# Spreading the four input deviations: one float32 matmul, or two of a rounded part and a rest

## The reference

```python
def rmsnorm(x, w):
    xf = x.astype(jnp.float32)
    y = xf * lax.rsqrt(jnp.mean(xf * xf, axis=-1, keepdims=True) + EPS)
    return (y * w.astype(jnp.float32)).astype(x.dtype)

def trunk(x, p):
    for layer in range(DEPTH):
        i = layer // 2
        h = rmsnorm(x, p['norm_w'][layer, 0])
        ...
        x = x + rmsnorm(m, p['norm_w'][layer, 1])
        h = rmsnorm(x, p['norm_w'][layer, 2])
        f = conv_ffn(h, p['ffn_w_in'][layer], p['ffn_conv_w'][layer], p['ffn_conv_b'][layer], p['ffn_w_out'][layer])
        x = x + rmsnorm(f, p['norm_w'][layer, 3])
    return x
```

## Time and profile before

| what | value |
|---|---|
| median of 3 runs | 1378.53 us (1378.49 to 1379.01) |
| the profiled execution | 1378.49 us |
| its span in the trace | 1376.7 us |
| PE busy | 1354.2 us, 98% of the span |
| DVE busy | 821.7 us, 60% |
| ACT busy | 641.7 us, 47% |
| POOL busy | 635.7 us, 46% |
| spread matmuls (L455) | 8 records, 592 ns each in the median |

### The profile page before, as it was taken

The page is one execution under the profiler, slowest core; times in us unless marked ns, Lnnn a source line. Parts: engine busy times, 40 slices in busy tenths (PEclk is TensorE's granted clock), DMA queues, the critical chain, the costliest instruction groups (busy, mean ns, idle before and its releaser), DMA issues.

```text
span 1376.7 us, 16583 instructions
## 1 busy us (share of the span) xinstructions
PE 1354.2 (98%) x6642; PEld 1122.5 (82%) x6642; DVE 821.7 (60%) x977; ACT 641.7 (47%) x1017; POOL 635.7 (46%) x304
## 2 busy tenths in 40 slices
PE   7999999999999999999999999999999999999997
PEld 6878767878898888888889877897898888888886
DVE  5657696760078998885001654477279998883003
ACT  6553885553345454444223475553545444443221
POOL 2344693226514554445454253563525544445550
PEclk9999999999999999999999999999999999999998
DMA  6332101123313332332333323211322333332321
GB/s 210 94 94 78 37 1 39 31 89 96 92 56 118 103 92 92 100 96 85 100 98 94 101 62 93 92 32 46 121 79 92 99 100 92 94 99 86 98 84 62
DMA packets 36765, 117.89 MB, mean 86 GB/s; under 512 B 3856, under 2 KB 8336, under 8 KB 36688
## 3 DMA queue, kind: packets, MB, share of 16 engines
q1 hardware_dynamic: 35744, 114.38, 26.8%
q10 hardware_dynamic: 944, 2.45, 0.6%
HBM read 114.58 MB, written 2.10 MB: 85 GB/s over the span
## 4 chain that ended last, share of the span: by engine, by line
PE 90%; DVE 4%; ACT 3%; POOL 2%; issue 0%; DMA 0%; DVEq 0%; ACTq 0%
PE bank L327 27%; PE bank L329 26%; PE bank L328 26%; PE bank L1350 1%; PE bank L1353 1%; PE bank L1174 1%; PE bank L1881 1%; PE bank L1378 1%; PE bank L1899 1%; POOL ebuf L1010 1%; ACT ebuf L1098 1%; DVE xres L583 1%; POOL ebuf L1006 1%; PE bank L1600 0%; PE bank L418 0%; DVE xw_lo L602 0%
## 5 line engine op out<-in xcount | busy, mean ns | idle before, releaser
L310 POOL TENSOR_TENSOR wlo<-raw,whi 128x1024 fp32r<-128x1024 f32 (+2 forms) x215 | 525.3, 2457 | 660.9 <-ACT whi L304 660.6
L327 PE MATMUL bank<-xw_hi,whi 128*128 128x512 f32 (+1 forms) x1344 | 510.4, 380 | 9.9 <-DVE xw_lo L602 8.2
L329 PE MATMUL bank<-xw_hi,wlo 128*128 128x512 f32 (+1 forms) x1344 | 500.3, 372 | 0.0
L328 PE MATMUL bank<-xw_lo,whi 128*128 128x512 f32 (+1 forms) x1344 | 500.0, 372 | 0.0
L304 ACT ACTIVATE whi<-raw 128x1024 fp32r<-128x1024 f32 (+2 forms) x217 | 221.1, 1024 | 208.7 <-DMA raw<-in_fout 113.6
L327 PEld LDWEIGHTS bank<-xw_hi,whi 128*128 128x128 f32 x1344 | 254.2, 189 | 60.0 <-issue 14.0
L328 PEld LDWEIGHTS bank<-xw_lo,whi 128*128 128x128 f32 x1344 | 254.1, 189 | 47.4 <-issue 3.5
L329 PEld LDWEIGHTS bank<-xw_hi,wlo 128*128 128x128 f32 x1344 | 253.9, 189 | 45.5
L555 DVE RECIPROCAL small<-small 128x2 f32<-128x2 f32 (+1 forms) x12 | 2.0, 169 | 328.1 <-ACT small L487 318.2
L660 DVE SCALAR_TENSOR_TENSOR cbuf<-ubuf,par,cbuf 128x510 f32<-128x510 f32 x100 | 170.8, 1708 | 3.5
L656 DVE SCALAR_TENSOR_TENSOR cbuf<-ubuf,par,cbuf 128x510 f32<-128x510 f32 x100 | 156.7, 1567 | 0.9 <-ACT cbuf L690 0.6
(11 more groups left out here) (251 smaller groups left out, 1432.8 us busy)
## 6 DMA issues: line engine op xcount, KB each, us to landing
raw<-in_fin SPq DMA_DIRECT2D x88, 512.0 KB, 3.6
raw<-in_fout SPq DMA_DIRECT2D x32, 448.0 KB, 3.3
raw<-in_gin SPq DMA_DIRECT2D x25, 512.0 KB, 3.6
raw<-in_hin SPq DMA_DIRECT2D x24, 512.0 KB, 3.6
raw<-in_hout SPq DMA_DIRECT2D x16, 512.0 KB, 3.6
raw<-in_fout SPq DMA_DIRECT2D x16, 512.0 KB, 3.5
raw<-in_gout SPq DMA_DIRECT2D x8, 512.0 KB, 3.7
xres<-in_x SPq DMA_DIRECT2D x8, 256.0 KB, 6.3
```

Of the source, the lines that this page charges most:

```text
L310: engine.tensor_tensor(wlo[s][:, 0:n], raw[s][:, 0:n], whi[s][:, 0:n].bitcast(F32), ALU.subtract).then_inc(w_lo, 1)
L327: first = nc.tensor.matmul(out_ap, wh, ah, start=start, stop=False)
L328: nc.tensor.matmul(out_ap, wh, al, start=False, stop=False)
L329: return first, nc.tensor.matmul(out_ap, wl, ah, start=False, stop=stop)
```

## The change

The four reciprocals are split as the weights are: DVE rounds them to float32r (`parts_r[:, 0:4]`), subtracts that from the reciprocals (`parts_r[:, 4:8]`), and makes two sets of diagonals, `res_diag0` and `res_diag1`, both 128x512 float32r. PE adds up two float32r matmuls in `bank6`, with a rounded all-ones matrix `ones_r`. `res_diag0` lies at the address of `ubuf1` and `res_diag1` at that of `cbuf1`. `ones_r` and `parts_r` are new memory of 136 columns in all, and the tensors allocated after them move up by that. One more DVE instruction at the start fills `ones_r`, and PE's first matmul waits for it (`ones_set` 2).

```diff
+        parts_r = sb("parts_r", 8, F32R)
+        ones_r = sb("ones_r", P, F32R)
...
         def pe_res_spread(pe, k):
-            pe.wait_ge(sem("res_dg"), of("res_dg", k) + 1)
-            nc.tensor.matmul(bank[6][:], ones[:, 0:P], ubuf[1][:], start=True, stop=True).then_inc(sem("res_sp"), 1)
+            pe.wait_ge(sem("res_dg"), 2 * of("res_dg", k) + 2)
+            nc.tensor.matmul(bank[6][:], ones_r[:], res_diag[0][:], start=True, stop=False)
+            nc.tensor.matmul(bank[6][:], ones_r[:], res_diag[1][:], start=False, stop=True).then_inc(sem("res_sp"), 1)
...
-            dve_diagonal(dve, slice(12, 16), ubuf[1][:], ("res_sd", of("res_sd", k) + 1),
-                         ("res_rs", of("res_rs", k) + 1), "res_dg")
+            rs = small[:, 12:16]
+            dve.wait_ge(sem("res_sd"), of("res_sd", k) + 1)
+            nc.vector.reciprocal(rs, rs).then_inc(sem("res_rs"), 1)
+            dve.wait_ge(sem("res_rs"), of("res_rs", k) + 1)
+            nc.vector.tensor_copy(parts_r[:, 0:4], rs).then_inc(sem("res_part"), 1)
+            dve.wait_ge(sem("res_part"), 2 * k + 3)
+            nc.vector.tensor_tensor(parts_r[:, 4:8], rs, parts_r[:, 0:4].bitcast(F32), ALU.subtract).then_inc(
+                sem("res_part"), 1)
+            for i in range(2):
+                if i:
+                    dve.wait_ge(sem("res_part"), 2 * k + 4)
+                nc.vector.tensor_tensor(res_diag[i][:].rearrange("p (b x) -> p b x", x=P),
+                                        parts_r[:, 4 * i:4 * i + 4].bitcast(F32).unsqueeze(2).broadcast_to([P, 4, P]),
+                                        ident[:].unsqueeze(1).broadcast_to([P, 4, P]), ALU.mult).then_inc(
+                                            sem("res_dg"), 1)
...
         def pe_start(pe, banks):
-            pe.wait_ge(sem("ones_set"), 1)
+            pe.wait_ge(sem("ones_set"), 2)
...
             dve.wait_ge(sem("ones_set"), 1)
+            nc.vector.tensor_copy(ones_r[:], ones[:, 0:P]).then_inc(sem("ones_set"), 1)
             dve_start(dve)
```

More of the change, by code:

```diff
@@ L122, in build_program @@
         sqacc = sb("sqacc", T)
-        ubuf = [sb(f"ubuf{i}", T) for i in range(2)]
+        ubuf, res_diag = [sb("ubuf0", T)], []
+        with ExitStack() as s:
+            res_diag.append(sb("res_diag0", T, F32R, s))
+        ubuf.append(sb("ubuf1", T))
         with ExitStack() as s:
@@ L130, in build_program @@
             kk1 = sb("kk1", NREQ * NCH * SEQ, F32, s)
-        cbuf = [sb(f"cbuf{i}", T) for i in range(4)]
+        cbuf = [sb("cbuf0", T)]
+        with ExitStack() as s:
+            res_diag.append(sb("res_diag1", T, F32R, s))
+        cbuf += [sb(f"cbuf{i}", T) for i in range(1, 4)]
         par = sb("par", NPARAM)
```

## The result

The changed kernel takes 1397.26 us in the median (1396.72 to 1397.67, 4 runs) against 1378.68 before: ratio 1.0132, 95% interval 1.0118 to 1.0145. The range of the prediction ended at 1382.3.

The account below looks back on a forecast made before the run. PE carries 90% of the chain that ended last; POOL holding DVE's second diagonals makes PE wait. 0.67 + 0.67 + 1.52 - 0.40 = 2.46 us on 1378.5 gives 1381.0 us, range 1378.6 to 1382.3.

Parts of the forecast that it names:

- the last sentence on other edits: Allocation: the shift of later tensors by 136 columns costs nothing; no row for it.
- the 0.06 for something unseen: Anywhere in the kernel: chance 0.06 left for something that the prediction doesn't see.
- PE's part: Float32 spread on PE becomes two float32r matmuls: 0.69 us with an ordinary one, saving 0.40 per place without a wait.
- the fourth place: Reciprocal at 1022.54: POOL comes after the second diagonals have started, so no wait and PE saves 0.40 us.
- the work on DVE: After each reciprocal: cast 0.184, two small operations 0.17 each, first diagonals at r + 0.49, second at r + 1.09.
- POOL's hold: POOL's weight subtraction blocks DVE's second diagonals, ending 2.80 us after the first, at the first three places; costs 0.67, 0.67, 1.52.
- POOL wins a tie: Second place: POOL at r + 1.11 against DVE at r + 1.09, yet DVE is held, ending at 416.93.
- The two outcomes: Second place held (forecast, 1381.0 us, chance 0.38) or not, with only two places held (1379.9 us, chance 0.27).
- The rival of the clock: PE's clock falls during its wait of about 2 us at the third place: 1383.0 us, chance 0.04.
- The rule on the ports: DVE and POOL share an exclusive port lock; whoever starts first has it. By it the second place isn't held, 1.07 lower.
- The row at 426: Trace before: DVE's operation starts at 426.15, POOL's at 426.18, DVE's is held 2.97 us; the forecast followed it.

Follow-up runs that it names:

- the kernel with the tensors on top: Changed kernel with ones_r and parts_r allocated above all other tensors, so no other tensor moves against the kernel before; 1380.74 us, ratio 1.0013.

## Why the prediction was wrong, and where it was right

- **The step that failed** is the last sentence on other edits: the shift of later tensors by 136 columns was cost at nothing, without a row. It is worth 16.7 us of the 18.6 by the kernel that has the shift alone (ratio 1.0121). With it 24 matmuls of 512 columns with weights from slots 0 to 3 take 5.60 us in place of 5.44, because it changes the distance between the two operands from a multiple of 256 bytes to 32 past one. No rival covered it but the 0.06 for something unseen, and the range took its bounds from other terms. The rows for a bound were in the trace: blocks of equal work in slots 4 and 5 took 0.16 us more than in slots 2 and 3. 3279 of the 4404 matmuls of full width don't use slots 4 and 5. They are as many as 137 blocks of 24, and 0.16 us on each would have given 22 us as an estimate from above.
- **Right: PE's part.** At the fourth place two spread matmuls and an ordinary one take 0.70 us (1039.62 to 1040.32), against 0.69 forecast.
- **Right: the work on DVE.** Cast 0.17, subtraction 0.16, first diagonals 0.50 behind the reciprocal (forecast 0.49), and the cast of the third place held by the end of a POOL operation (0.11 against 0.16).
- **Right: POOL's hold** at the first and third place. The second diagonals are done at 32.67 (forecast 32.66), PE follows 0.05 and 0.06 behind them (forecast 0.05), and the places cost +0.68 and +1.45 against +0.67 and +1.52. The fourth place is free, -0.35 against -0.40; the slower pace takes the difference of the last.
- **Wrong: "POOL wins a tie".** At the second place the second diagonals and POOL's subtraction were 0.01 us apart, and DVE got through: the two sets took 1.29 us together, and POOL's operation, at 417.81, took 2.93 in place of 2.38. The second set alone:

```profile
417.80 0.69 DVE L633 TENSOR_TENSOR res_diag<-parts_r,ident 128x512 fp32r<-128x512 f32 x1
```

In the kernel with the tensors on top three places were held, and at the second of them POOL started 1.06 us behind the reciprocal, not 1.12. That is ahead of the second set, which starts 1.1 behind it. DVE, then POOL, in that kernel:

```profile
413.95 0.18 DVE L626 RECIPROCAL small<-small 128x4 f32<-128x4 f32 x1 [2.59 <-ACT small L526]
...
414.45 3.50 DVE L635 TENSOR_TENSOR res_diag<-parts_r,ident 128x512 fp32r<-128x512 f32 x2
```

```profile
415.01 2.39 POOL L320 TENSOR_TENSOR wlo<-raw,whi 128x1024 fp32r<-128x1024 f32 x1 [3.96 <-ACT whi L314]
```

So a few hundredths of a us decide this place, and which way they fall is luck. The two outcomes had 0.38 and 0.27, and 1.07 us between them, which was the right way to carry it.

- **The rival of the clock** didn't come about: PE stood still for 1.55 us at the third place, and in the 4 us from 792.65 on the granted clock is 1.00. The price of this rival rested on the slow start, but both stretches of the start show a granted clock of 1.00 in the earlier trace rows, so no row shows that the clock made the start slow.
- **The rule on the ports.** The block of DVE by POOL is as the Trainium skill, SBUF — State Buffer, section "SBUF: two separate sides", has it, and at the second place DVE started first (417.80 against 417.81) and got through, as that section of the Trainium skill says. In the kernel with the tensors on top POOL started first and DVE was held, which fits it too. The row at 426 doesn't: DVE's operation is recorded 0.03 us ahead of POOL's there, and was held.

## What to carry to other kernels

When an edit allocates memory, list what moves, and compute the distance between the two operands of the hot matmuls before and after; where one can choose, make it a multiple of 256 bytes. A sum over the changed lines is only the half of a prediction: a price on an unchanged instruction, times its count, needs a row too, here blocks of the same work in two places of the memory. When a trace shows the lag growing in a stretch with no wait in it, count instructions in equal windows before looking for a cause.

## What the hardware showed

The pace of a 512-column float32r matmul with its 128-column weight load depends on the distance between the addresses of the two operands: 0.2267 us (5.44 for 24) at a multiple of 256 bytes, and up to 0.2333 (5.60), 3% more, at the four other distances that were tried. It is the distance, since moving both by 32 bytes changed nothing. The period of 256 bytes rests on the pairs 0 and 256, 128 and 384, and 192 and 448. At a distance of 64 the pace was not always the same. That the two reads get in each other's way is what this suggests; no run measured it apart from the pace.

The Trainium skill, TensorE: Matmul & The Clock Gate, section "Step-by-step: what each phase is for", says that moving operand and weights are read through two independent ports and that a weight load takes no read bandwidth from the running matmul. By that one wouldn't expect the distance to matter. The measurements here say that for these operands it does, by up to 3% (5.44 against 5.60 us for 24 matmuls).
